# The second block's residual, norms and output projections with tokens on the partitions, its gates as rows read back from a DRAM scratch

## The chip, the cores and the metric

One core of one Trainium2 chip runs the whole model part in one launch. The metric is the device time of one execution in microseconds (us), the median of several executions. Smaller is better.

## The reference

256 tokens of width 1024 pass through two stacked blocks, all in fp32. The first block has two layers of hybrid mixer, memory attention and SwiGLU, each followed by a layer norm. The change leaves its arithmetic alone. The second block runs over a context stream of 256 tokens and over the latents (the first block's output), with adaptive modulation. Cut to what matters here:

```python
def rmsnorm(x, g):
    return x * rsqrt(mean(x * x, axis=-1) + EPS) * g
def modulate(h, shift, scale):
    return h * (1.0 + scale) + shift

for l in range(2):
    sh1, sc1, g1, sh2, sc2, g2 = split(silu(c) @ ada_w[l] + ada_b[l], 6)
    # csh1 ... cg2 in the same way from c_ctx
    h_lat = modulate(rmsnorm(x, norm1_g[l]), sh1, sc1)
    h_ctx = modulate(rmsnorm(ctx, norm1_g[l]), csh1, csc1)
    ...                                   # keys and values of both, attention, branches
    x = x + g1 * (merged @ w_out[l])                             # mixer projection
    h2 = modulate(rmsnorm(x, norm2_g[l]), sh2, sc2)
    x = x + g2 * (hidden(h2) @ ffn_down[l])                      # ffn-down projection
    if l == 0:
        ...                               # the same two updates for ctx, with cg1 and cg2
return x
```

So the second block has six gated residual updates (context layer 0, latent layers 0 and 1; mixer and ffn-down each). Five of them are followed by an rms norm inside the block, and the last one is the output.

## The kernel before

**Products.** The fp32 weights come from DRAM as units of 128x1024 on SyncE's queue into seven `raw` buffers. ScalarE (ACT) copies a unit into `whi`, its high part (L1397, in `hi_part`), GpSimd (POOL) subtracts to get `wlo` (L606), and TensorE (PE) makes each product from three passes: high weight times high input, high weight times low input, low weight times high input. There are four `whi`/`wlo` slots (`SLOTS`). The copy of unit s waits for the raw unit and for unit s-4 to have been used. The order on every engine is written out by hand: PE, ACT and DVE each run through a program of their own, and semaphores join them.

**Two orientations.** With features on the partitions (feature-major) the weights are stationary and 256 tokens are streamed, so a unit is 24 matmuls of 256 columns (`wide_unit`, L640, L641, L644). With tokens on the partitions (token-major) 128 tokens are stationary and 512 weight columns are streamed, so a unit is 12 matmuls of 512 columns (`rows_unit`, L694, L695, L698).

**The first block** has its residual stream token-major already. Its mixer-out and ffn-down projections use `rows_unit`. The last two units go through `last_rows`, which finishes the 256x1024 result piece by piece, (token tile, half) = (0,0), (0,1), (1,0), (1,1). Of these, the first two release `tiles_done` and the last two `units_used`. VectorE (DVE) adds each piece to `x` and takes its statistics (L2026, L2034), ACT takes the root (L1421) and scales 128x256 pieces into `normal` (`normalise`, L1444), PE transposes them (`turn_first`: 8 transposes, `turn_second`: 2 each, L792), ACT writes the high inputs with gain and shift (L1450), and DVE the low ones (L2061, L1964).

**The second block** is feature-major. `mixer_out` and `ffn` use `wide_unit`, the last two units `last_blocks` (four groups of two output tiles, each done before the next begins). `gated_residual` (L2499) is one operation for each of the eight 128x256 tiles: aux times the gate, a per-partition scalar, plus `x`. Then `rms` follows. ACT squares (L1744), PE sums over the partitions (L1200, L1192, L1205), ACT takes the root (L1421), DVE the reciprocal (L2051), PE spreads it (`spread_inverse`, L846), with five `keep_busy` matmuls (L1185) in the waits, and DVE scales each tile (L2480), ACT writes the high input (L1738) and DVE the low one (L2486). The next chunk starts at L657, on `first_hi`, with the first tile.

The latents' first norm of the second block is spread over the context's layer 1: its sums are `latent_sums` (L832). Before it, at the end of the first block, `last_norm` turns the first block's output to feature-major by 16 transposes, and DVE writes `x` (L2069). `DIFF_BEFORE_T` and `DIFF_BEFORE_V` say how many weight units PE works off as cover before each attention step's transposes and values (L1248 among the latter's).

Of the kernel before, what the change touches and what calls it, by code (L numbers as in the profile page):

```python
# [56 lines left out]
PARTS = (0, 1), (2, 3), (4, 5), (6,), (7,)  # L57
# [4 lines left out]
DIFF_BEFORE_T = [1] * STEPS  # L62
DIFF_BEFORE_V = [1, 2, 1, 1] * (STEPS // 4)
# [217 lines left out]
def build(nc, a, split, n_first):  # L281
# [4 lines left out]
    with ExitStack() as ctx:  # L286
# [44 lines left out]
        rows_used = sem("rows_used")  # L331
        ln_var = sem("ln_var")
# [204 lines left out]
        x_first, ln_rows, normal = zt(X_FIRST, 8), zt(LN_ROWS, 8), zt(NORMAL, 8)  # L537
# [17 lines left out]
        def token_moments(tt):  # L555
            return small[:, 88 + 2 * tt:90 + 2 * tt]
# [9 lines left out]

        def scaled_tile(k):
            return aux[:, (2, 3, 1)[k % 3], 0:T]
# [4 lines left out]
        def _(sp):  # L573
# [21 lines left out]
            for q in range(4):  # L595
                sp.wait_ge(out_ready, t.next(out_ready, 2))
                sp.dma_start(a["out"][:, quarter(q)], x[:, quarter(q)]).then_inc(out_sent, 16)
# [11 lines left out]
        def _(pe):  # L609
# [141 lines left out]
            def aux_tile(j):  # L751
                return aux[:, j // 2, (j % 2) * T:(j % 2 + 1) * T]

# [27 lines left out]
            def first_rows(second_half):  # L781
# [8 lines left out]
            def turn(tt, tiles):  # L790
                for k in tiles:
                    mm = pe.transpose(normal_tile(k)[:, tt * P:(tt + 1) * P], normal[:, tt * D + k * P:tt * D + (k + 1) * P], ident)  # L792
                return mm

            def turn_first():
                pe.wait_ge(resid_ready, t.next(resid_ready))
                pe.wait_ge(normal_ready, t.next(normal_ready, 4))
                turn(0, TILES)

            def turn_second(q):  # L800
                pe.wait_ge(normal_ready, t.next(normal_ready))
                turn(1, (2 * q, 2 * q + 1)).then_inc(normal_turned, 1)


            def last_blocks(out, k, h, src):
                xh, xl = src
                wh, wl, low = next_unit()
                low_part(low)
# [2128 lines left out]
```

## Time and profile before

| what | value |
|---|---|
| median of 3 executions | 2621.76 us (2621.74 to 2623.76) |
| profiled execution | 2620.55 us |
| its span (first to last instruction) | 2618.8 us |
| TensorE busy | 2594.7 us, 99% |
| GpSimd busy | 1951.5 us, 75% |
| ScalarE busy | 1431.0 us, 55% |
| VectorE busy | 1213.6 us, 46% |
| granted TensorE clock over the span | 1.000 |

The span is the stretch from the first to the last instruction of the profiled execution. An engine is busy while an instruction of it runs. TensorE's matmuls are pipelined: a matmul's own duration is longer than the distance at which they start, so a run of matmuls is costed by the distance between starts.

### The profile page before, as it was taken

The numbers are of one execution on the slowest core, as the hardware profiler recorded it, in microseconds if no ns is written. First come the engines' busy times: TensorE is split into PE (matmuls) and PEld (weight loads), VectorE is DVE, ScalarE is ACT, GpSimd is POOL, SyncE is SP. The second block draws the span as 40 slices with busy tenths as digits, with TensorE's granted clock in tenths as the row PEclk, the third lists the DMA queues.
The fourth block names the chain that finished last, engine by engine and source line by source line (L and its number), as shares of the span: only waits on it lengthen the run. The fifth ranks groups of instructions, "written<-read, shape, count | busy, mean of one in ns | idle before, by whom it ended". The sixth has DMA issues, their size and how long they took to land.

```text
span 2618.8 us, 42331 instructions
## 1 busy us (share of the span) xinstructions
PE 2594.7 (99%) x16735; PEld 2241.7 (86%) x16735; DVE 1213.6 (46%) x2311; ACT 1431.0 (55%) x2024; POOL 1951.5 (75%) x816
## 2 busy tenths in 40 slices
PE   8999999999999999999999999999999999999999
PEld 8877888889778788888889988887899988878898
DVE  3443462254434553424426552555355554542655
ACT  5756654456565644555654445556554455565443
POOL 6667678876577598786778877865778877568787
PEclk9999999999999999999999999999999999999999
DMA  7556575575566655654455556544445565345453
GB/s 295 211 221 251 165 278 193 188 279 191 212 216 219 257 194 193 236 186 151 163 177 170 189 174 215 191 137 137 164 155 196 185 217 175 133 133 178 165 189 129
DMA packets 139942, 504.60 MB, mean 193 GB/s; under 512 B 15584, under 2 KB 17760, under 8 KB 138080
## 3 DMA queue, kind: packets, MB, share of 16 engines
q1 hardware_dynamic: 132912, 481.57, 53.2%
q10 hardware_dynamic: 6832, 20.32, 2.2%
q8 instruction: 133, 2.18, 0.3%
q14 instruction: 65, 0.53, 0.1%
HBM read 498.68 MB, written 3.15 MB: 192 GB/s over the span
## 4 chain that ended last, share of the span: by engine, by line
PE 94%; DVE 2%; ACT 2%; DVEq 1%; issue 0%; DMA 0%; ACTq 0%; SPq 0%; POOL 0%
PE lin L856 13%; PE lin L644 12%; PE lin L694 12%; PE lin L698 11%; PE lin L695 11%; PE lin L640 5%; PE lin L641 4%; PE aux L644 3%; PE aux L641 3%; PE aux L640 3%; PE aux L695 2%; PE aux L694 2%; PE aux L698 2%; PE aux L1241 1%; PE aux L1259 1%; PE aux L939 1%
## 5 line engine op out<-in xcount | busy, mean ns | idle before, releaser
L606 POOL TENSOR_TENSOR wlo<-raw,whi 128x1024 fp32r<-128x1024 f32 x812 | 1951.3, 2422 | 657.3 <-ACT whi L1397 648.7
L1397 ACT ACTIVATE whi<-raw 128x1024 fp32r<-128x1024 f32 x811 | 845.1, 1057 | 627.6 <-PE lin L698 267.7
L856 PE MATMUL lin<-in_both,whi 128*128 128x512 f32 x1600 | 400.7, 392 | 0.3
L694 PE MATMUL lin<-whi,in_both 128*128 128x512 f32 x942 | 378.1, 401 | 1.5 <-DVE Z L2563 1.2
L695 PE MATMUL lin<-whi,in_both 128*128 128x512 f32 x942 | 367.8, 390 | 0.0
L644 PE MATMUL lin<-in_both,wlo 128*128 128x256 f32 x2560 | 364.4, 283 | 0.3 <-POOL wlo L606 0.3
L644 PEld LDWEIGHTS lin<-in_both,wlo 128*128 128x128 f32 x2560 | 344.8, 191 | 16.4 <-POOL wlo L606 0.7
L856 PEld LDWEIGHTS lin<-in_both,whi 128*128 128x128 f32 x1600 | 289.8, 189 | 55.0 <-DVEq L2441 0.9
L698 PE MATMUL lin<-wlo,in_both 128*128 128x512 f32 x944 | 253.6, 390 | 0.0
L2426 DVE TENSOR_REDUCE Z<-lin 128x512 f32<-128x1024 f32 x100 | 122.4, 1224 | 269.0 <-PE lin L644 267.2
L640 PE MATMUL lin<-in_both,whi 128*128 128x256 f32 x920 | 234.0, 290 | 8.5 <-ACT whi L1902 6.8
L641 PE MATMUL lin<-in_both,whi 128*128 128x256 f32 x920 | 227.9, 284 | 0.0
L694 PEld LDWEIGHTS lin<-whi,in_both 128*128 128x128 f32 x942 | 176.9, 188 | 57.2 <-ACT whi L1397 10.2
L698 PEld LDWEIGHTS lin<-wlo,in_both 128*128 128x128 f32 x944 | 177.1, 188 | 37.8 <-POOL wlo L606 0.3
L695 PEld LDWEIGHTS lin<-whi,in_both 128*128 128x128 f32 x942 | 177.1, 188 | 34.1
L640 PEld LDWEIGHTS lin<-in_both,whi 128*128 128x128 f32 x920 | 176.8, 192 | 21.9 <-issue 10.9
L641 PEld LDWEIGHTS lin<-in_both,whi 128*128 128x128 f32 x920 | 177.0, 192 | 0.3
L694 PE MATMUL lin<-whi,br_hi 128*128 128x512 f32 x360 | 143.7, 399 | 0.0
L695 PE MATMUL lin<-whi,br_lo 128*128 128x512 f32 x360 | 140.5, 390 | 0.0
L640 PE MATMUL aux<-br_hi,whi 128*128 128x256 f32 x528 | 131.4, 283 | 0.0
L641 PE MATMUL aux<-br_lo,whi 128*128 128x256 f32 x528 | 131.4, 283 | 0.0
L1714 ACT ACTIVATE Z<-lin 128x256 f32<-128x256 f32 x60 | 23.1, 384 | 177.4 <-DVEq L2430 177.4
(317 smaller groups left out, 3823.6 us busy)
## 6 DMA issues: line engine op xcount, KB each, us to landing
raw<-in_wstream SPq DMA_DIRECT2D x907, 512.0 KB, 3.3
Z<-in_ln_rows ACTq DMA_DIRECT2D x5, 1024.0 KB, 9.3
gate_row<-in_gate_bias ACTq DMA_DIRECT2D x12, 256.0 KB, 3.2
Z<-in_rel ACTq DMA_DIRECT2D x2, 1536.0 KB, 11.4
Z<-in_mem_t ACTq DMA_DIRECT2D x2, 1024.0 KB, 7.1
kv_store<-Z ACTq DMA_DIRECT2D x2, 1024.0 KB, 8.4
Z<-kv_store ACTq DMA_DIRECT2D x2, 1024.0 KB, 10.7
x<-in_x_tok SPq DMA_DIRECT2D x1, 1024.0 KB, 5.5
```

Of the source, the lines that this page charges most:

```text
L606: pool.tensor_tensor(wlo[s][:, :], raw[i % RAWS][:, :], whi[s][:, :].bitcast(F32), ALU.subtract).then_inc(lo_pool, 1)
L640: pe.matmul(out, wh, xh, start=start, stop=False, skip_group_check=True)
L641: pe.matmul(out, wh, xl, start=False, stop=False, skip_group_check=True)
L644: return pe.matmul(out, wl, xh, start=False, stop=stop, skip_group_check=True)
L694: pe.matmul(out, xh, wh, start=start, stop=False, skip_group_check=True)
L695: pe.matmul(out, xl, wh, start=False, stop=False, skip_group_check=True)
L698: return pe.matmul(out, xh, wl, start=False, stop=stop, skip_group_check=True)
L856: pe.matmul(lin[:, p, up * CH:(up + 1) * CH], wh[:, w], in_both[:, :, k * T:(k + 1) * T], start=(k == 0), stop=(k == KD - 1), skip_group_c ...
L939: mm = pe.matmul(score(g)[tt], q[:, tt * P:(tt + 1) * P], k[:, 0:(tt + 1) * P], start=True, stop=True)
L1241: mm = pe.matmul(aux[:, m, 0:kts * P], q, head_keys(m, h, kts), start=True, stop=True)
L1397: act.activation(whi[s % SLOTS][:, :], raw[i % RAWS][:, :], ACT.Copy).then_inc(hi_ready, 1)
L2426: i = dve.tensor_reduce(three(u, 2), both.rearrange("p a (s t) -> p a t s", s=2), AX.X, ALU.add)
```

## The change

The residual of the second block becomes token-major. Part by part:

- Mixer-out and ffn-down in all three layers of the second block use `rows_unit` and `last_rows`. `wide_unit`, `last_blocks` and `mixer_out` go.
- A gate is now a row along the free axis. For each layer ACT stores both gates to a DRAM scratch (`store_gates`, 2 DMAs, pieces of four values) and loads them back broadcast over the partitions (`load_gates`, 3 DMAs). They lie in the scratch with the feature tile innermost, so DVE reads a gate at a step of four values.
- `gated_residual` is per 128x512 piece a multiplication in place in PSUM and an addition, with a settle behind each. `rms_inverses(0)`, a wait for ACT's root and a reciprocal, stands between the pieces (1,0) and (1,1).
- ACT takes the squares with their sum (`square`), the roots, and scales 128x256 pieces by the inverse (`scale_pieces`). PE turns them (`block_turns`, the last four transposes behind the next chunk's first two units). ACT and DVE modulate the turned tiles.
- PE's sums, `spread_inverse` and three of the five `keep_busy` matmuls go.
- `last_norm` keeps the token-major `x`: its transposes and feature-major tiles go, the row operations of the other norms (`token_rows`) and their 1 MB load take their place. The context is loaded token-major as well (1 MB more).
- `latent_sums` becomes `latent_turns`, 16 transposes.
- One weight unit of the attention's cover moves from before `T(12)` to before `V(11)`.
- The output is token-major and leaves in four quarters, as before, each after one piece.

```diff
-DIFF_BEFORE_T = [1] * STEPS
-DIFF_BEFORE_V = [1, 2, 1, 1] * (STEPS // 4)
+DIFF_BEFORE_T = [1] * 12 + [0] + [1] * 3
+DIFF_BEFORE_V = [1, 2, 1, 1] * 2 + [1, 2, 1, 2] + [1, 2, 1, 1]
...
-            def wide_unit(out, k, kn, src):
-                xh, xl = src
-                wh, wl, low = next_unit()
-                for j in range(KD):
-                    high_product(out(j), wh[:, j * P:(j + 1) * P], tile(xh, k), tile(xl, k), k == 0 and j % 2 == 0)
-                low_part(low)
-                for j in range(KD):
-                    mm = low_product(out(j), wl[:, j * P:(j + 1) * P], tile(xh, k), k == kn - 1)
-                mm.then_inc(units_used, 1)
...
+            def block_turns():
                 pe.wait_ge(lin_free[0], t.ahead(lin_free[0]))
                 keep_busy(2)
-                spread_inverse(0)
-                keep_busy(3)
+                turn_first(block_normal)
+                keep_busy(2)
+                turn_second(0, block_normal)
+                turn_second(1, block_normal)
+            turns_behind = {0: lambda: turn_second(2, block_normal), 1: lambda: turn_second(3, block_normal)}
...
-                mixer_out(lambda: merged_transposes(1))
-                rms()
-                ffn()
+                mixer_rows(lambda: merged_transposes(1))
+                block_turns()
+                ffn(turns_behind)
...
+            def square(src, tt, h, done=None):
+                if done:
+                    act.wait_ge(done, t.next(done))
+                act.activation(token_piece(block_normal, tt, h), token_piece(src, tt, h), ACT.Square, accum_out=piece_squares(tt, h))
+                act.drain()
+                if h:
+                    root(token_std[:, tt:tt + 1], piece_squares(tt, 1), rms_std, 1.0 / D, 0, root_shift(tt))
+                else:
+                    act.activation(root_shift(tt), piece_squares(tt, 0), ACT.Identity, bias=eps[:, 1:2], scale=1.0 / D)
+                    act.drain()
+            def rms(l, x, i, then=None):
+                square(x, 0, 0, resid2)
+                square(x, 0, 1, resid2)
+                square(x, 1, 0, resid2)
+                scale_pieces(x, 0, 0, 2)
+                square(x, 1, 1, resid2)
+                scale_pieces(x, 0, 2, 4)
+                scale_pieces(x, 1, 0, 2)
+                modulated_hi(l, i, 0)
...
+            def store_gates(layer, l, params):
+                act.wait_ge(params_ready, params)
+                stored = a["gate_store"][2 * layer:2 * layer + 2, :].rearrange("g (h p k) -> p g h k", h=2, p=P)
+                for g in range(2):
+                    act.dma_start(stored[:, g], mod[l][:, 24 * g + 16:24 * g + 24].rearrange("p (h k) -> p h k", h=2)).then_inc(gates_stored, 16)
...
-            def gated_residual(l, x, gate, done=resid2):
-                for h in range(2):
-                    for q in quarters_done(2 * h):
-                        for k in (2 * q, 2 * q + 1):
-                            xs = x[:, k * T:(k + 1) * T]
-                            dve.scalar_tensor_tensor(xs, aux[:, k // 2, (k % 2) * T:(k % 2 + 1) * T], mod[l][:, gate + k:gate + k + 1], xs,
-                                                     ALU.mult, ALU.add).then_inc(done, 1)
-                settle()
+            def gated_residual(x, gate, done=resid2):
+                for tt in range(2):
+                    for h in range(2):
+                        if tt:
+                            chunk_done(1)
+                        else:
+                            dve.wait_ge(tiles_done, t.next(tiles_done))
+                        y, xs = rows_bank(tt, h), token_piece(x, tt, h)
+                        tt_(three(y, 4), three(y, 4), gate(h), ALU.mult)
+                        settle()
+                        tt_(xs, y, xs, ALU.add).then_inc(done, 1)
+                        settle()
+                        if tt and h == 0 and done is resid2:
+                            rms_inverses(0)
+                if done is resid2:
+                    settle().then_inc(resid_ready, 1)
+                    rms_inverses(1)
```

How the programs stand against each other at the context's layer 0, between the mixer's projection and the ffn. On PE, before, from the projection's last matmul to the first of the next chunk (`aux` and `lin` are PSUM, `Z` the squares, `c` and `zero_w` constants):

```order
L644 MATMUL aux<-in_both,wlo 128x256
L1200 MATMUL aux<-Z,c 32x256 x6
L1192 MATMUL aux<-c,Z 128x1 x2
L1205 MATMUL aux<-share,probs 128x1 x2
L1192 MATMUL aux<-c,Z 128x1 x2
L1185 MATMUL lin<-zero_w 128x512 x2
L846 MATMUL aux<-c,small 128x128 x2
L1185 MATMUL lin<-zero_w 128x512 x3
L657 MATMUL lin<-in_both,whi 128x256 x4
```

The same place on PE in the changed kernel (`Z` is now the scaled tokens, L794 the transposes, L672 the next chunk's first matmuls):

```order
L713 MATMUL aux<-wlo,in_both 128x512
L1151 MATMUL lin<-zero_w 128x512 x2
L794 MATMUL aux<-c,Z 128x128 x8
L1151 MATMUL lin<-zero_w 128x512 x2
L794 MATMUL aux<-c,Z 128x128 x4
L672 MATMUL lin<-in_both,whi 128x256 x4
L659 MATMUL lin<-in_both,wlo 128x256 x4
```

The sums and the spreading went, and 12 transposes stand ahead of the chunk in their place. Four more follow behind its first two units.

On ACT, before, at the same place (L1397 copies weights, L1744 squares, L1421 is the root, L1738 writes the high inputs):

```order
L1397 ACTIVATE whi<-raw 128x1024 x5
L1744 ACTIVATE Z<-Z 128x512 x3
L1744 ACTIVATE Z<-Z 128x256 x2
L1421 ACTIVATE small<-aux,eps 128x2
L1738 ACTIVATE in_both<-aux,mod 128x256 x4
```

And in the changed kernel (L1353 copies weights, L1398 squares with their sum, L1403 prepares the root and L1377 takes it, L1411 scales, L1712 writes the high inputs):

```order
L1353 ACTIVATE whi<-raw 128x1024 x5
L1398 ACTIVATE Z,small<-Z 128x512
L1403 ACTIVATE small<-small,eps 128x1
L1398 ACTIVATE Z,small<-Z 128x512
L1377 ACTIVATE small<-small 128x1
L1398 ACTIVATE Z,small<-Z 128x512
L1403 ACTIVATE small<-small,eps 128x1
L1411 ACTIVATE Z<-Z,small 128x256 x2
L1398 ACTIVATE Z,small<-Z 128x512
L1377 ACTIVATE small<-small 128x1
L1411 ACTIVATE Z<-Z,small 128x256 x4
L1712 ACTIVATE in_both<-aux,mod,mscale 128x256 x2
```

Between the fifth weight copy and the first high input there were five squares and a root. Now there are four squares, four small operations and six scalings.

## Rows read from the trace of the kernel before

**Rows 1.** The page: busy time of each engine; the chain by engine

```profile
PE 2594.7 (99%) x16735; PEld 2241.7 (86%) x16735; DVE 1213.6 (46%) x2311; ACT 1431.0 (55%) x2024; POOL 1951.5 (75%) x816
PE 94%; DVE 2%; ACT 2%; DVEq 1%; issue 0%; DMA 0%; ACTq 0%; SPq 0%; POOL 0%
```

**Rows 2.** Groups of PE by form: count, then busy us, mean ns

```profile
L640 PE MATMUL aux<-br_hi,whi 128*128 128x256 f32 x528 | 131.4, 283 | 0.0
L640 PE MATMUL aux<-in_both,whi 128*128 128x256 f32 x192 | 49.1, 284 | 0.0
```

**Rows 3.** Timeline of PE: first high matmuls of three units; start us, us

```profile
1342.11 0.39 PE L694 MATMUL lin<-whi,br_hi 128*128 128x512 f32 x1
...
1344.83 0.28 PE L640 MATMUL aux<-in_both,whi 128*128 128x256 f32 x1
...
1347.70 0.28 PE L640 MATMUL aux<-in_both,whi 128*128 128x256 f32 x1
```

**Rows 4.** Timeline of the context's norm between mixer and ffn

```profile
1366.10 1.06 ACT L1397 ACTIVATE whi<-raw 128x1024 fp32r<-128x1024 f32 x1 [1.82 <-PE aux L644]
...
1368.60 0.28 PE L644 MATMUL aux<-in_both,wlo 128*128 128x256 f32 x1
...
1372.99 0.86 ACT L1738 ACTIVATE in_both<-aux,mod 128x256 fp32r<-128x256 f32 x2 [1.24 <-DVE aux L2480]
...
1373.61 0.35 PE L657 MATMUL lin<-in_both,whi 128*128 128x256 f32 x1 [0.53 <-ACT in_both L1738]
```

**Rows 5.** Timeline of two token-major norms of the first block

```profile
885.46 1.63 PE L792 MATMUL aux<-c,Z 128*128 128x128 f32 x10 [1.43 <-ACT Z L1444]
...
1074.70 1.06 ACT L1397 ACTIVATE whi<-raw 128x1024 fp32r<-128x1024 f32 x1 [1.72 <-PE aux L698]
...
1075.57 0.39 PE L698 MATMUL aux<-wlo,br_hi 128*128 128x512 f32 x1
...
1078.30 2.08 ACT L1444 ACTIVATE Z<-x,small 128x256 f32<-128x256 f32 x4 [2.20 <-DVEq L2047]
...
1084.30 1.03 PE L792 MATMUL aux<-c,Z 128*128 128x128 f32 x8
```

**Rows 6.** Prices on ACT and DVE: groups by form; two timeline rows

```profile
L1744 ACT ACTIVATE Z<-Z 128x512 f32<-128x512 f32 x6 | 3.5, 620 | 0.4 <-DVE Z L2499 0.4
L1421 ACT ACTIVATE small<-small,eps 128x1 f32<-128x1 f32 x12 | 3.4, 285 | 1.3 <-DVEq L2039 1.2
...
1706.32 0.64 ACT L1780 ACTIVATE aux<-aux,small 128x512 f32<-128x512 f32 x1
...
1706.98 0.65 ACT L1780 ACTIVATE aux<-aux,small 128x512 f32<-128x512 f32 x1
...
L1964 DVE TENSOR_TENSOR lin<-lin,Z 128x512 f32<-128x512 f32 x16 | 10.4, 694 | 0.6
L2026 DVE SCALAR_TENSOR_TENSOR x<-x,aux 128x512 f32<-128x512 f32 x16 | 10.9, 682 | 21.5 <-PE aux L698 20.6
L1964 DVE TENSOR_TENSOR in_both<-Z,in_both 128x512 fp32r<-128x512 f32 x6 | 9.9, 1675 | 6.2 <-ACT in_both L1418 6.1
```

**Rows 7.** Timeline of PE at the start of the program

```profile
6.76 0.56 PE L640 MATMUL lin<-in_both,whi 128*128 128x256 f32 x1 [6.76 <-ACT whi L1902]
...
9.46 0.41 PE L640 MATMUL lin<-in_both,whi 128*128 128x256 f32 x1
9.67 0.36 PE L641 MATMUL lin<-in_both,whi 128*128 128x256 f32 x1
```

**Rows 8.** Timeline of ACT behind five DMA issues, latent layer 0

```profile
1621.66 2.01 ACT L1397 ACTIVATE whi<-raw 128x1024 fp32r<-128x1024 f32 x2 [5.55 <-issue]
```

**Rows 9.** Timeline of PE: the latents' sums

```profile
1600.35 1.07 PE L832 MATMUL aux<-Z,c 128*32 128x256 f32 x16
```

**Rows 10.** Timeline of DVE: the last residual operations

```profile
2615.33 0.88 DVE L2499 SCALAR_TENSOR_TENSOR x<-aux,mod,x 128x256 f32<-128x256 f32 x2 [0.56 <-PE aux L644]
```

**Rows 11.** Waits of PE: us in total, times, longest

```profile
PE aux L1248 <- DVE probs L2628: 1.5, 2, 0.8
```

More of the change, by code:

```diff
@@ L863, in gate_up, with ffn @@
                         after[k0]()
-            def ffn(after=(), context_norm=False, rows=False):
+            def ffn(after=(), context_norm=False):
                 def down(c):
@@ L868, in down @@
                         pe.wait_ge(hid_lo, t.next(hid_lo))
-                    if rows:
-                        rows_unit(rows_bank, c % 6, c == 0, (br_hi, br_lo))
-                        return
-                    wh, wl, low = next_unit()
-                    high, lower = hidden_tile(br_hi, c), hidden_tile(br_lo, c)
-                    for j in range(KD):
-                        high_product(aux_tile(j), wh[:, j * P:(j + 1) * P], high, lower, c == 0 and j % 2 == 0)
-                    low_part(low)
-                    for j in range(KD):
-                        mm = low_product(aux_tile(j), wl[:, j * P:(j + 1) * P], high, False)
-                    mm.then_inc(units_used, 1)
+                    rows_unit(rows_bank, c % 6, c == 0, (br_hi, br_lo))
                 feature_chunk(0, fresh=TILES, after=after)
@@ L895, in ffn @@
                 pe.wait_ge(hid_lo, t.next(hid_lo, 2))
-                if rows:
-                    last_rows(rows_bank, (HIDDEN - 2) % 6, (br_hi, br_lo))
-                for h in range(0 if rows else 2):
-                    last_blocks(aux_tile, (HIDDEN - 2) % 6, h, (br_hi, br_lo))
+                last_rows(rows_bank, (HIDDEN - 2) % 6, (br_hi, br_lo))
             def modulation_tile(out, u, first, last):
@@ L1145, in first_layer @@
                 last = l == L - 1
-                ffn(columns_behind(fill), last, True)
+                ffn(columns_behind(fill), last)
                 if last:
@@ L1170, in last_norm @@
                 advance(fill, 3)
-                advance(units, 1)
-                turn_first()
-                advance(units, 1)
-                for q in range(4):
-                    turn_second(q)
+                advance(units, 2)
                 advance(fill, 1)
@@ L1437, in token_root, with scale_pieces @@
                 root(token_std[:, tt:tt + 1], token_moments(tt)[:, 1:2], ln_std, 1.0, 0)
+            def square(src, tt, h, done=None):
[8 more added lines that the diff above has]
+                    act.drain()
+            def scale_pieces(src, tt, first, last):
+                if first == 0:
+                    act.wait_ge(rms_inverse, t.next(rms_inverse))
+                for q in range(first, last):
+                    c = slice(tt * D + q * T, tt * D + (q + 1) * T)
+                    act.activation(block_normal[:, c], src[:, c], ACT.Copy, scale=token_scale(tt)).then_inc(normal_ready, 1)
             def normalise(tt, first, last):
@@ L1941, in _ @@
                 modulated_hi(0, 0, k)
+            hi_part()
             evacuate(1, 1, zt(VL + 4, 4))
[L1943 to L1944 removed]
+            for k in range(4, KD):
+                modulated_hi(0, 0, k)
             act.drain().then_inc(kv_copied, 1)
@@ L2325, in first_layer @@
                 residual(rows_bank)
-                rows = norm_with_modulation(l, "ln_ffn", ADA_LN_FFN, not last)
-                if not last:
-                    run(rows)
+                run(norm_with_modulation(l, "ln_ffn", ADA_LN_FFN, not last))
             def context_inverse():
```

240 lines of the change are left out of this document (110 added, 130 removed).

## The prediction

> **What bounds the kernel now.** I read the page first. TensorE is busy 2594.7 of 2618.8 us and makes 94% of the chain that ended last, the other engines have slack [rows 1]. So a change is worth what it takes from TensorE's work, plus what it does to the few stretches where TensorE waits. The table of PE's waits has only short ones past the start (such as [rows 11]), except where the program itself leaves PE with filler. Those places are the norms of the second block. In the timeline of the context's norm the projection's last matmul starts at 1368.60 and its slot of 0.12 ends at 1368.72 (this is T0 below). The next chunk's first matmul starts at 1373.61 [rows 4]. That is 4.9 us in which PE does only sums, spreading and keep-busy matmuls. It is paid five times: context mixer to ffn, start of context layer 1, latent 0 mixer to ffn, start of latent 1, latent 1 mixer to ffn. There the chain is residual, squares, sums, root, spreading, scaling, high input, first matmul. So I cost two things: the projections' matmuls, and the length of that chain.
>
> **Projections.** Before, a 256-column unit takes 1347.70 - 1344.83 = 2.87 us from first matmul to first matmul (24 at 0.12), and a 512-column unit takes 1344.83 - 1342.11 = 2.72 us (12 at 0.227) [rows 3]. There are 528 + 192 = 720 high matmuls at eight to a unit, so 90 units (three layers with 22 + 8) [rows 2]. Each saves 0.15: **-13.6 us**, all on PE's path.
>
> **The norm's new chain, from T0.** Pieces end at -4.1, -2.7, -1.4 and 0 (a quarter of two units, 1.36, apart).
> - DVE takes per piece a multiplication and an addition, 0.69 and 0.68 [rows 6], with settles of about 0.05 each: 1.45. It keeps up. The last piece, behind the wait for the first tile's root (2.2, below) and its reciprocal, is added by about 3.9.
> - ACT is the question. Its fifth weight copy waits for a slot. Before, half of the last two units was freed 2.6 us ahead of T0 (1366.10 against 1368.72). In `last_rows` both are held until the third piece is done. The first block shows that: 1074.70 against a last matmul that starts at 1075.57 [rows 5]. So the copy runs from -1.1 to about 0, and every square stands behind it, though the first two pieces were ready long before.
> - A square with its sum is 0.66 (starts 1706.32 and 1706.98, an exponential of the same size with its sum; the plain square has 0.62), a 128x1 operation 0.285 [rows 6], and I take 0.1 for a drain. Two pieces of one token tile are then 1.10 + 1.05. A scaling of 256 columns has a cadence of 0.50 (four in 2.08, the last 0.59) [rows 5].
> - In program order: squares of tile 0 until 2.2, square (1,0) 3.3, two scalings 4.3, square (1,1) with root 5.4, two scalings 6.45, two more 7.4. PE's eight transposes start at 6.5 and take 0.9 (8 in 1.03, the last one's latency off [rows 5]), two keep-busy matmuls bring it to 7.9, two transposes 8.1, ACT's first high input (0.59 by the 256-column scaling) 8.8, the first fresh matmul about 8.9.
>
> Against 4.9 that is +4.0, five times: **+20 us**. No PE work lies beside it: unlike the first block's norms, `block_turns` has only 4 keep-busy matmuls.
>
> **Behind it in the chunk.** Four transposes, about 0.45. DVE's path to the low input is a pass longer (`tensor_scalar` and subtraction, where one operation stood). A 256-column pass takes 0.44 (two in 0.88 [rows 10]), so the low inputs come about 0.5 later, and DVE then needs about 0.95 for a tile where PE needs 1.44: a wait at the first tile or two, 0.7 in all. Five times 1.15: **+5.8 us**.
>
> **The latents' first norm.** 16 transposes, about 1.9 us, and perhaps 1 us of wait, against sums of about 1.5 (the largest of them 1.07 [rows 9]): **+1.4**. **`last_norm`** loses 16 transposes, two runs of eight at 1.03 with latency [rows 5]: **-1.9**. Its DVE work (token rows, more than the tiles it replaces) and its 1 MB load lie beside the second block's first chunks, and I put them at 0. What they need late is the context's residual only, hundreds of us on.
>
> **The end.** The last two tiles take 0.88 on DVE behind the last matmul [rows 10]. The new piece takes 1.45: **+0.5**. The output's transfers stay.
>
> **The clock.** At the program's start PE idles for 6.76 us and then starts 256-column matmuls 0.21 us apart until 9.67 (9.46 and 9.67 [rows 7]), where 0.12 is the full rate [rows 3]: the 1.2 GHz level for 14 matmuls, 1.3 us lost. Nowhere else is PE idle over 1.5 us (1.43 at 885.46 [rows 5], without a slow stretch behind it). The new norm leaves PE idle from about 0.5 to 6.5, nearly as long as at the start, with ten small matmuls to follow. I take the same 1.3 us for each, on transposes, keep-busy matmuls and first tiles: **+6.5**. The bounds are 0 and 1.9 (transposes slowed inside the chain as well) each, 0 to 9.5.
>
> The Trainium skill states the same rule ("TensorE: Matmul & The Clock Gate", section "Why this matters for your kernels"): gaps between bursts of matmuls put the engine back to the lower clock. By it all five norms lose clock. The start's rows agree, though they show a cold start and not a gap in a run, which is why the term has a chance and isn't taken as sure.
>
> **Gates.** DVE reads the gate at a step of four values. The trace has no such read. Below: it costs as the contiguous one, 0.69. Above: as a 512-element pass with two SBUF operands and POOL beside it, 1.68 [rows 6], so +1 per piece. As ACT binds until the squares of tile 1, the first three pieces have cover; only the last piece (needed at 4.3) and the end of the kernel would feel it: up to +0.7 five times and +1 three times, +6. I take 0.
>
> The Trainium skill ("SBUF — State Buffer", section "Specifications (TRN2)") says that each access which crosses to a new 16-byte line pays a penalty. A step of four fp32 values does that each time, so by it the multiplication is slower than the contiguous one.
>
> The DMAs for the gates are five more issues on ACT per layer. At the start of latent layer 0 five issues in a row kept ACT from everything else for 5.55 us, and no wait of PE followed, since four slots of weights stand between [rows 8]. The two stores join exactly that crowd, 2.2 us at 1.1 each: 0 to 2.2 more for PE. I take 0, as now. The moved unit of cover stands at a place where PE waits up to 0.8 now [rows 11]: -0.8 to +1.5, taken as 0.
>
> **Sum.** -13.6 + 20 + 5.8 + 1.4 - 1.9 + 0.5 = +12.2, with the clock +18.7. On the profiled execution's 2620.55 that is 2632.8 and 2639.3. The median of the runs is 1.2 above it: 2634.0 and **2640.5 us**.
>
> **Rivals.**
> - *Chain as forecast, no clock drop*: 2634. For it: the granted clock reads 1.000 over the whole span although the start is slow, so the rows tell little of the gate, and the keep-busy matmuls stand on both sides. Chance 0.22.
> - *The other side, the chain stays short*: if the weight copy were not late, ACT had the first three squares behind it before T0, and the last piece bound: 1.45 for DVE, square and root 1.05, reciprocal with its settle 0.2, one scaling 0.5, transposes 0.3, high input 0.6, first matmul 0.1, so 4.2 to 4.6, as short as today's 4.9. At 4.6 the sum is -13.6 - 1.9 + 1.4 + 0.5 + 5 x (1.15 - 0.3) = -9.3, **2612**. The sign turns where a norm is 1.6 us longer than today, since 5 x (1.6 + 1.15) makes up the 13.6 that is left without the norms. Against it: from the end of the copy ACT's own work alone is 7.4, whatever DVE does. Chance 0.15, and 0.08 more for a case between, within 0.2%.
> - *A slower multiplication, gate DMAs or attention cover on top*: 2640 + 6 to 10, **2648**. Chance 0.15.
> - The change does what it says as far as the order shows, so a case of "nothing happens" isn't among them.
>
> My forecast (chain and clock) has 0.40. From the cases: faster by over 0.2% (5 us, about what a measurement of this kernel can tell) 0.15, within it 0.08, slower 0.77. For 8 in 10 the range drops the fast rival and the far end: **2621 to 2651**. The likeliest case alone would have 2635 to 2646.
>
> **What the profile after would show.** Units of the projections 2.72 apart. The fifth weight copy ending at about T0, the last scaling ahead of the first high input ending near +7.4, PE idle of about 6 us before the eight transposes, released by ACT's scaling. First fresh matmul at +8.9. Behind it matmuls of 256 columns 0.21 apart for some 3 us if the clock fell, 0.12 if not. Multiplication by the gate near 0.69. I am wrong if the gap is under 7 us (squares ahead of the copy, or drains and sums cheaper), if PE has waits elsewhere that I put at 0, or if the gate's read is far above 0.69.

## The result and the profile after

The changed kernel takes **2651.43 us** (median of 4, 2650.92 to 2651.85), the kernel before 2621.99 us beside it. The ratio is 1.0113, with a 95% interval of [1.0101, 1.0125]: slower by 29.4 us. The sign was forecast. The time lies 0.4 us above the stated range, and the loss is 1.6 times the 18.7 that were forecast. The profiled span is 2648.9 us against 2618.8, so 30.1 us are to be found.

The page after, its busy line and its chain, beside [rows 1]:

```profile
PE 2585.9 (98%) x15578; PEld 2190.2 (83%) x15578; DVE 1243.1 (47%) x2307; ACT 1459.5 (55%) x2109; POOL 1954.1 (74%) x816
PE 92%; DVE 2%; ACT 2%; DMA 1%; POOL 1%; DVEq 1%; ACTq 1%; issue 0%; SPq 0%
```

TensorE is busy 9 us less, and the kernel is 30 us longer: the loss is idle time. The changed kernel's waits of PE (us in total, times, longest) say where:

```profile
PE aux L794 <- ACT Z L1411: 29.5, 6, 5.7
...
PE lin L709 <- ACT whi L1353: 4.5, 2, 3.4
PE lin L837 <- DVEq L2431: 3.4, 3, 1.1
...
PE lin L713 <- POOL wlo L621: 1.8, 5, 0.5
```

Five waits of 5.7 us stand ahead of the eight transposes of the five norms. This is the timeline of the context's norm after, at the place of [rows 4]:

```profile
1368.40 1.06 ACT L1353 ACTIVATE whi<-raw 128x1024 fp32r<-128x1024 f32 x1 [3.02 <-PE aux L713]
...
1369.28 0.39 PE L713 MATMUL aux<-wlo,in_both 128*128 128x512 f32 x1
1369.37 0.61 ACT L1398 ACTIVATE Z<-Z 128x512 f32<-128x512 f32 x1
...
1373.04 0.69 DVE L1966 TENSOR_TENSOR Z<-aux,Z 128x512 f32<-128x512 f32 x1
1373.77 0.63 ACT L1398 ACTIVATE Z<-Z 128x512 f32<-128x512 f32 x1
...
1374.76 1.69 ACT L1411 ACTIVATE Z<-Z,small 128x256 f32<-128x256 f32 x4
...
1375.80 1.94 PE L794 MATMUL aux<-c,Z 128*128 128x128 f32 x8 [5.68 <-ACT Z L1411]
1377.53 1.06 PE L1151 MATMUL lin<-zero_w 128*128 128x512 bf16 x2
1378.38 1.06 PE L794 MATMUL aux<-c,Z 128*128 128x128 f32 x4
...
1379.76 0.71 PE L672 MATMUL lin<-in_both,whi 128*128 128x256 f32 x4 [0.32 <-ACT in_both L1712]
```

The last slot ends at T0 = 1369.51. The fifth weight copy ends at T0, the squares follow in a row, and the transposes start at +6.3, as forecast. But the eight then take 1.94 us where the first block's take 1.03 [rows 5], the filler 1.06, and the first fresh matmul comes at **+10.25** (forecast 8.9, before 4.9). The reason shows in the windows of that norm (the busy times, then the granted clock, DMA share and GB/s at the end):

```profile
1369.50:1372.60 3.10, 0.61 (x3) 0.12 (x2) 2.63 (x4) 2.54 (x9) 2.37 (x1) 1.00 0.33 128
1372.70:1379.40 6.70, 3.60 (x14) 2.74 (x14) 1.12 (x3) 3.96 (x11) 0.00 (x0) 0.50 0.24 79
1379.50:1384.00 4.50, 4.01 (x31) 3.82 (x32) 3.63 (x8) 3.54 (x8) 1.20 (x1) 0.99 0.02 4
```

The granted clock fell to 0.50 (1.2 GHz) 2.6 us into the idle stretch, and it was back at 2.4 GHz 0.2 us before the first fresh matmul. All five norms have such a slow stretch of 6.8 us, beginning 2.6 to 4.7 us into the idle time. In the other four it ends behind the first fresh matmul: 0.1 us behind it at the start of latent layer 1, and 1.7 to 1.9 us in three norms. Two windows around its end in the second norm, where the first fresh matmul starts at 1575.76:

```profile
1577.25:1577.50 0.25, 0.25 (x2) 0.25 (x1) 0.25 (x1) 0.25 (x2) 0.00 (x0) 0.50 0.00 0
1577.50:1577.75 0.25, 0.25 (x2) 0.17 (x2) 0.25 (x2) 0.25 (x2) 0.00 (x0) 0.92 0.00 0
```

The first fresh matmul comes at +10.25 in all five, so most of the loss lies on the norm's own chain. What the slow clock costs in the chunk behind is priced with e1_busy below.

**Where the 30.1 us are.** The start of the same PE work in both traces, subtracted, gives a shift; its growth between two places is what that stretch costs.

| stretch | forecast | measured |
|---|---|---|
| `last_norm` and the context's first chunks (shift +2.0 at 1220) | -1.9 | +2.0 |
| projections, 90 units at 0.15 | -13.6 | -13.6 |
| the five norms, T0 to first fresh matmul (10.25 - 4.89 each) | +20 and clock 6.5 | +26.8 |
| chunks behind four of the norms (three ffns 1.9, 2.0, 2.1; latent 1 1.1) | +4.6 | +7.1 |
| chunk behind the context's second norm, latents' norm | +1.2 and +1.4 | +2.0 |
| start of latent layer 0 | 0 | +4.7 |
| moved cover (the two waits of 0.8 at L1248 [rows 11] are gone) | 0 | -1.8 |
| behind the last matmul | +0.5 | +2.9 |

They sum to 18.7 and 30.1.

### The profile page after: what moved, and what is told of

Its sections match the earlier page's. It is cut to its first block, busy times and chain, and to the rows that moved or that the text cites. A ratio compares the mean times of both kernels' runs of the same rounds, so it can differ in the third digit from the quotient of the medians.

```text
span 2648.9 us, 40235 instructions
## 1 busy us (share of the span) xinstructions
PE 2585.9 (98%) x15578; PEld 2190.2 (83%) x15578; DVE 1243.1 (47%) x2307; ACT 1459.5 (55%) x2109; POOL 1954.1 (74%) x816
## 4 chain that ended last, share of the span: by engine, by line
PE 92%; DVE 2%; ACT 2%; DMA 1%; POOL 1%; DVEq 1%; ACTq 1%; issue 0%; SPq 0%
PE lin L837 13%; PE lin L709 11%; PE lin L659 11%; PE lin L713 11%; PE lin L710 11%; PE aux L710 5%; PE aux L709 5%; PE aux L713 5%; PE lin L655 4%; PE lin L656 4%; DMA raw<-in_wstream 1%; PE aux L1190 1%; PE aux L1208 1%; PE aux L907 1%; PE aux L875 1%; PE aux L794 1%
## 5 line engine op out<-in xcount | busy, mean ns | idle before, releaser
L1353 ACT ACTIVATE whi<-raw 128x1024 fp32r<-128x1024 f32 x811 | 845.2, 1057 | 621.3 <-PE lin L713 266.1
L710 PE MATMUL aux<-whi,br_lo 128*128 128x512 f32 x440 | 172.5, 392 | 0.0
L709 PE MATMUL aux<-whi,br_hi 128*128 128x512 f32 x440 | 172.2, 391 | 0.0
L713 PE MATMUL aux<-wlo,br_hi 128*128 128x512 f32 x440 | 122.5, 389 | 0.0
```

The source lines that it names most:

```text
L709: pe.matmul(out, xh, wh, start=start, stop=False, skip_group_check=True)
L710: pe.matmul(out, xl, wh, start=False, stop=False, skip_group_check=True)
L713: return pe.matmul(out, xh, wl, start=False, stop=stop, skip_group_check=True)
L1353: act.activation(whi[s % SLOTS][:, :], raw[i % RAWS][:, :], ACT.Copy).then_inc(hi_ready, 1)
```

## The experiments

All medians are of 4 to 11 executions, beside the kernel before on the same chip (2621.2 to 2622.0).

### e1_busy: no idle stretch ahead of the transposes

```diff
                 pe.wait_ge(lin_free[0], t.ahead(lin_free[0]))
-                keep_busy(2)
+                keep_busy(26)
                 turn_first(block_normal)
```

> Edit: 26 instead of 2 filler matmuls ahead of the eight transposes, in each of the five norms, so that PE has no idle stretch there. Clock theory: the eight transposes take about 1.06 instead of 1.94 and the filler behind them 0.6 instead of 1.06, the first fresh matmul comes 8.9 instead of 10.25 behind the projection's end, the granted clock is 1.000, and the time falls by about 5 x 1.35 = 6.8, to 2644.7. Rival (the slow stretch is harmless since most of it lies in idle time, the chain on ACT sets the gap): no change, 2651. Rival (the filler's 5.7 us reach past the ready transposes): slower by up to 0.3 a norm.

Measured: 2643.38 us, 8.1 less than the changed kernel. The timeline of PE at the same norm:

```profile
1368.45 0.39 PE L713 MATMUL aux<-wlo,in_both 128*128 128x512 f32 x1
1368.68 5.79 PE L1151 MATMUL lin<-zero_w 128*128 128x512 bf16 x26
1374.99 1.06 PE L794 MATMUL aux<-c,Z 128*128 128x128 f32 x8 [0.52 <-ACT Z L1411]
1375.89 0.59 PE L1151 MATMUL lin<-zero_w 128*128 128x512 bf16 x2
1376.32 0.60 PE L794 MATMUL aux<-c,Z 128*128 128x128 f32 x4
1377.45 0.71 PE L672 MATMUL lin<-in_both,whi 128*128 128x256 f32 x4 [0.53 <-ACT in_both L1712]
```

The transposes take 1.06 and the gap is 8.77, the forecast's 8.9. The clock theory holds: with PE busy the norms have no slow stretch, and 1.48 us come back in each. The other 3.9 per norm are the chain itself, as forecast. Behind the third and the fifth norm, where the changed kernel's slow stretch reached 1.7 and 1.9 us into the chunk, the work up to the next norm or the end is only 0.20 and 0.25 us shorter here. (The profile has one slow stretch elsewhere, at 1636, behind the wait of 3.5 us at the start of latent layer 0. The changed kernel's profile has none there, and the work around it is 2.2 us longer here.)

### e2_order: ACT's work in another order

The fifth weight copy moves from ahead of the squares to behind the scalings, and the first tile's scalings to ahead of the last square:

```diff
-                hi_parts(5)
+                hi_parts(4)
                 rms(l, x, 1, ACT.Silu)
...
                 square(x, 0, 1, resid2)
-                square(x, 1, 0, resid2)
                 scale_pieces(x, 0, 0, 2)
-                square(x, 1, 1, resid2)
+                square(x, 1, 0, resid2)
                 scale_pieces(x, 0, 2, 4)
+                square(x, 1, 1, resid2)
                 scale_pieces(x, 1, 0, 2)
+                hi_part()
```

> Edit on ACT alone: the fifth weight copy is issued behind the scalings instead of ahead of the squares, and all four scalings of the first token tile stand ahead of the last square. Theory (ACT's order of work sets the gap): the eight transposes start about 4.5 us behind the projection's end instead of 6.3, the first fresh matmul 1.3 to 1.8 us earlier in each norm, together 2651.4 - 5 x 1.35 = 2644.7. Rival (DVE, at 1.9 us for each piece, has become the bound): the last piece is added 4.2 behind the end whatever ACT does, and the gap shrinks by under 0.5 each, 2649 or more. Rival (the next chunk then waits for the weight that is copied late): no gain.

Measured: 2645.99 us, 5.4 less, between the theory (2644.7) and its rival (2649). The gap shrank to 9.1 to 9.5, by 0.8 to 1.1 each. The order matters, but the first square of the second half isn't free: the second piece is added on DVE only at T0, and DVE's reciprocal stands behind the third piece's addition (1.9 us a piece).

### e3_issues: DMA issues behind the weight copies

The two gate stores and the load of the context rows are issued behind the layer's gelu instead of at its start.

```diff
-                store_gates(layer, l, (1, 3, 4)[layer])
                 act.dma_start(zt(S2, 2), a["sgu_w"][l * P:(l + 1) * P, :]).then_inc(sgu_landed, 16)
...
                 act.drain().then_inc(gelu_ready, 1)
+                store_gates(layer, l, (1, 3, 4)[layer])
+                if not layer:
+                    act.dma_start(context, a["ctx_tok"]).then_inc(ctx_tok_landed, 16)
```

> Edit: the stores of the gates and the load of the context rows are issued later in a layer, behind the copies of the first weights and the gelu. Theory (DMA issues in front of weight copies on ACT): the waits of 3.4 us at 1640 and of 1.0 us at 1094 go, 2651.4 - 4.4 = 2647.0, perhaps with 0.3 given back where the issues now stand. Rival (the transfers themselves are late or crowd the weights' queue): the waits stay or show as waits for raw, 2650 to 2651.

Measured: 2647.76 us, 3.7 less. This is what had happened in the changed kernel at the start of latent layer 0, where [rows 8] were free of a wait:

```profile
1633.77 2.55 ACTq L1739 DMA_DIRECT2D gate_store<-mod  x2
1636.34 1.35 ACTq L1820 DMA_DIRECT2D Z<-in_sgu_w  x1
1637.72 1.22 ACTq L1821 DMA_DIRECT2D Z<-in_sgu_b  x1
1638.97 0.46 ACTq L1822 DMA_DIRECT2D Z<-in_lam  x1
1639.54 3.90 ACT L1353 ACTIVATE whi<-raw 128x1024 fp32r<-128x1024 f32 x4 [6.93 <-issue]
...
1640.74 0.47 PE L709 MATMUL lin<-whi,in_both 128*128 128x512 f32 x1 [3.44 <-ACT whi L1353]
```

With the edit the wait is 1.59 and the one near 1094 (1.03) is 0.27. The rest of 1.59 is no matter of the gates: ACT reaches the remaining issues later against PE than in the kernel before (first store issued 7.5 us behind the chunk's first fresh matmul, where it was 3.1), since the last high inputs wait for transposes that stand behind PE's units. So the 3.44 are 1.85 for the two stores and 1.59 for the later place.

### e4_rows: the last norm's row operations later

```diff
-                run(norm_with_modulation(l, "ln_ffn", ADA_LN_FFN, not last))
+                rows = norm_with_modulation(l, "ln_ffn", ADA_LN_FFN, not last)
+                if last:
+                    return rows
+                run(rows)
...
                     qk_chunk(c, rotate, gating_lo if c == 0 else None)
+                    if not rotate and c < 3:
+                        advance(last_token_rows, (2, 1, 1)[c])
```

In this kernel the row operations read a normalised tile that the query chunks have written over by then, so the latents' values differ. The instructions and their sizes are the same.

> Edit on DVE alone: the four row operations of the first block's last norm run between the context's query and key chunks instead of beside its first chunk. Theory (they slow POOL's subtractions beside them from 2.4 to 2.9 to 3.3 us, with no spare slots at that place): the four waits of PE for wlo behind 1094 (0.55, 0.31, 0.33, 0.32) go, 2651.4 - 1.5 = 2649.9. Rival (the slots are short because ACT's copies start 1 us late there, whatever DVE does): the waits stay, 2651.4.

Measured: 2650.34 us, 1.1 less; the span is 1.5 less, and four waits for wlo behind 1094 are gone. In the changed kernel POOL's subtractions beside the row operations stand so:

```profile
1093.81 17.38 POOL L621 TENSOR_TENSOR wlo<-raw,whi 128x1024 fp32r<-128x1024 f32 x6 [8.31 <-ACT whi L1353]
...
1094.27 3.27 DVE L1966 TENSOR_TENSOR x<-x,Z 128x1024 f32<-128x1024 f32 x1
...
1096.51 1.20 PE L713 MATMUL lin<-wlo,in_both 128*128 128x512 f32 x4 [0.55 <-POOL wlo L621]
```

Six in 17.38 is 2.9 each, over the 2.72 in which PE uses a unit.

### e5_gate: the gates contiguous

```diff
-            return row.rearrange("p (f k) -> p k f", k=4)
+            return row.rearrange("p (k f) -> p k f", k=4)
...
-                stored = a["gate_store"][2 * layer:2 * layer + 2, :].rearrange("g (h p k) -> p g h k", h=2, p=P)
+                stored = a["gate_store"][2 * layer:2 * layer + 2, :].rearrange("g (h k p) -> p g h k", h=2, p=P)
```

> Edit: the gates lie in the scratch in plain feature order (the stores have pieces of one value), so DVE reads them contiguously. Theory (the step of four values costs 1.07 instead of 0.69 for each piece, and it counts only where DVE is last): the multiplication takes 0.69, the tail behind the last matmul shortens by about 1.5, the norms' gap stays at 10.25 since ACT is last there, 2651.4 - 1.6 = 2649.8. Rival (the slow gate read is what made the norms long): the gap shrinks by 0.4 to 1.5 in each, 2643 to 2648. Rival (1024 pieces of 4 bytes for each gate come late or hold ACT's queue): a new wait, 2651 or more.

Measured: 2663.86 us, 12.4 more. In the changed kernel the gate's read shows as

```profile
L1966 DVE TENSOR_TENSOR aux<-aux,ytok 128x512 f32<-128x512 f32 x12 | 12.8, 1068 | 30.7 <-PE aux L713 29.8
```

and here as 699 ns. The norms' gap went from 10.25 to about 9.9. But the stores of single values held ACT's queue in the context's layer 0. The two stores there in the changed kernel, then the same place here:

```profile
1090.14 0.94 ACTq L1739 DMA_DIRECT2D gate_store<-mod  x2
```

```profile
1089.11 5.33 ACTq L1739 DMA_DIRECT2D gate_store<-mod  x2
1094.47 4.30 ACTq L1820 DMA_DIRECT2D Z<-in_sgu_w  x1
1098.80 2.40 ACTq L1821 DMA_DIRECT2D Z<-in_sgu_b  x1
1101.23 0.46 ACTq L1822 DMA_DIRECT2D Z<-in_lam  x1
1101.78 3.90 ACT L1353 ACTIVATE whi<-raw 128x1024 fp32r<-128x1024 f32 x4 [11.43 <-issue]
...
1102.98 0.77 PE L709 MATMUL lin<-whi,in_both 128*128 128x512 f32 x1 [11.17 <-ACT whi L1353]
```

So the second rival was right: the stores in pieces of one value took 5.33 for two, against 0.94 with pieces of four, and the next issues were longer too. In the profile the first norm comes 8.8 later, and the stretches with the starts of the latents' two layers are 3.4 and 4.3 longer. The tail is 1.5 shorter, as the theory had it.

### e6_short: only what the first tiles need

```diff
+                pe.wait_ge(normal_ready, t.next(normal_ready, 2))
+                turn(0, (0, 1), block_normal)
                 keep_busy(2)
-                turn_second(0, block_normal)
-                turn_second(1, block_normal)
+                pe.wait_ge(resid_ready, t.next(resid_ready))
+                turn(0, (2, 3), block_normal)
+                pe.wait_ge(normal_ready, t.next(normal_ready, 2))
+                turn(1, (0, 1), block_normal).then_inc(normal_turned, 1)
+                pe.wait_ge(normal_ready, t.next(normal_ready))
+                turn(1, (2, 3), block_normal).then_inc(normal_turned, 1)
```

> Edit on ACT and PE: the fifth weight copy behind the first two high inputs, only the scalings that the first two feature tiles need ahead of them, PE turns those tiles as they come (2 + 2 + 2 + 2 transposes ahead of the chunk, the others in pairs behind its first two units). The gate's read stays at a step of four. Theory (the gap is the ordering of ACT's work plus the clock): the last piece is added 4.2 behind the end, its square, root and one scaling end at about 6.0, first fresh matmul near 7.0 instead of 10.25, 2651.4 - 5 x 3.2 = 2635. If PE's idle stretches of 2 to 3 us still bring the clock down, 0.5 to 1 more for each norm, 2638 to 2640. Rival (the chain has a floor of its own, drains and semaphores): gap above 8.5, 2643 or more.

Measured: 2642.79 us, 8.6 less where 11 to 16 were expected, though the gap did shrink to 7.5 (by 2.75 each). The stretches between the norms gave about 7 us back. The windows of its second norm show it (first fresh matmul at 1569.78):

```profile
1563.00:1566.00 3.00, 0.00 (x0) 0.00 (x0) 2.64 (x5) 1.95 (x6) 0.00 (x0) 1.00 0.38 150
1566.00:1569.70 3.70, 2.22 (x10) 1.25 (x10) 0.57 (x3) 3.11 (x9) 0.00 (x0) 0.67 0.00 0
1569.80:1572.80 3.00, 3.00 (x7) 2.42 (x8) 2.76 (x7) 3.00 (x7) 1.69 (x1) 0.50 0.00 0
1573.00:1576.00 3.00, 3.00 (x15) 2.44 (x14) 0.68 (x3) 1.83 (x4) 2.34 (x2) 0.82 0.50 157
```

The slow stretch began behind a shorter idle time, and then lasted into busy PE time (until 1574.09). So a shorter gap with the same slow stretch behind it can move the loss from idle time to work. Not all of the 7 us is shown to be that: 3.9 of them lie between the second and the third norm, where this profile also has the slow stretch at 1636 that e1_busy has and the changed kernel hasn't. How much is the clock's, e9_short_busy shows.

### e7_best: the edits together

The reordered norms, contiguous gates, later issues, and the row operations spread where their inputs still stand (two ahead of the context's gating, two behind its first query chunk).

> Edit: the reordered norms of the run before this one, the contiguous gates, the later DMA issues, and the last norm's row operations spread over the context's first chunks. Theory (all measured terms add up): the gap of a norm 5.5 to 6.0 (DVE's last piece at 1.6 to 2.2 behind the end), 2651.4 - 5 x 4.4 - 1.6 - 3.6 - 1.1 = 2623, the same as before the change within 0.2%; if the chunk's follow-up waits (1.1 three times) go too, 2620. Rival (another engine binds once these are gone): gap of 7 or more, 2630.

Measured: 2631.66 us (2628.77 to 2635.37), 19.8 less, ratio to before 1.0039 [1.0026, 1.0052]. That is 8.7 over the expected 2623. The gap is 5.9 to 6.4, above the 5.5 to 6.0 expected, and each norm still has a slow stretch.

### e8_proj: the kernel before with the new projections alone

```diff
-                    wide_unit(aux_tile, k, KD, (in_hi, in_lo))
+                    rows_unit(rows_bank, k, k == 0, (in_hi, in_lo))
...
-                for h in range(2):
-                    last_blocks(aux_tile, KD - 2, h, (in_hi, in_lo))
+                last_rows(rows_bank, KD - 2, (in_hi, in_lo))
```

> The kernel before, with one edit: the second block's projections run as 12 matmuls of 512 columns with tokens stationary, everything behind them unchanged (the residual then reads a transposed result, so the output isn't the reference's, the instructions and waits are those of before). It prices the first term alone. Theory (0.15 for each of 90 units, the norms about 0.5 longer as the last two slots come free later): 2622.0 - 13.6 + 0 to 2.5, 2608.4 to 2611. Rival (units come no faster since another engine paces them): over 2615.

Measured: 2613.45 us, ratio 0.9970 [0.9958, 0.9981], 8.2 less than before, over the expected 2611. Its profile says why: between two norms the 22 units of the context's ffn take 3.32 us less (0.15 each, the term is right), and the norms are 1.05 longer (gap 5.94; one of the five 6.22), twice what I had allowed for the later last slots.

### e9_short_busy, e10_best_busy: the same two with PE kept busy

The counts are 18 and 7 in e9_short_busy, 13 and 7 in e10_best_busy.

```diff
-                keep_busy(2)
+                keep_busy(18)
                 pe.wait_ge(normal_ready, t.next(normal_ready, 2))
                 turn(0, (0, 1), block_normal)
-                keep_busy(2)
+                keep_busy(7)
```

> Edit: the reordered norms of the run e6_short with 18 and 7 filler matmuls where they have 2 and 2. Theory (in e6_short the half-rate stretch of 3.4 or 6.8 us began later against the norm and so fell on the next chunk's matmuls, which gave back about 7 us of what the order had gained): with PE kept busy there is no slow stretch, the gap is 6.6 to 6.9 instead of 7.5, the chunks behind lose nothing, 2642.8 - 9 to 11 = 2632 to 2634. Rival (the loss behind the norms is ACT's and DVE's, not the clock's): only the gap shrinks, 2639 or more.

Measured: 2638.16 us, 4.6 less than e6_short, short of the expected 9 to 11. No norm has a slow stretch, but the gap stayed at 7.2 to 7.5, so PE's rate doesn't set it there. DVE's pieces do, as the next runs show. Of the 7 us that e6_short had lost between the norms, 4.0 came back. The other 3.4 stayed. Behind the first norm that is 0.4, the same in both runs, with no slow stretch behind it in either, so the rival was right for a part: some of the loss belongs to the new order of work on ACT and DVE. (One slow stretch of 3.4 us is left between the norms, at the start of latent layer 0.)

> Edit: e7_best with 13 and 7 filler matmuls where it has 2 and 2. Theory: gap 5.5 to 5.8 instead of 5.9 to 6.4, no slow stretch in or behind the norms, 2631.7 - 5 to 8 = 2624 to 2627, still slower than before the change by 0.1 to 0.2%, since the gap stays over the 4.9 of before and the transposes and waits of the chunks are extra. Rival (the spread of e7_best, 2628.8 to 2635.4, has another cause): no change, 2630.

Measured: 2626.81 us, 4.9 less than e7_best, ratio to before 1.0020 [1.0010, 1.0029]. No norm has a slow stretch, but the gap is 6.0 to 6.4 as in e7_best, and not the 5.5 to 5.8 of the theory. The two profiled executions differ by only 1.7, since e7_best's was its shortest (2628.77), so where the rest of the 4.9 lies isn't shown.

### e11_strided: the slow gate read in the short norm

> Edit: e10_best_busy with the gates back at a step of four values (stores with pieces of four values, 18 filler matmuls for 13). It prices the gate's read where DVE is last. Theory (0.38 for each piece, three to four pieces on the path of each norm and of the end): gap 1.0 to 1.3 longer five times, the tail 1.5, the small waits from the 4-byte stores about 1 less: 6 to 7 us over e10_best_busy. Rival (ACT is last even in the short norm): gap as in e10_best_busy, at most 2 us over it.

The kernel is e10_best_busy with the gates at a step of four again, and 18 filler matmuls for 13. Measured: 2631.95 us, 5.1 more than e10_best_busy, a little under the expected 6 to 7. The gaps are 7.2 to 7.5 against 6.0 to 6.4. Once ACT's order is short, DVE is last, and then the step of four counts in every norm. (The profiled execution was a long one, with a span of 2637.4 and a wait of 4.4 at 1129 behind a DVE operation that took 6.79 where e10_best_busy has 1.42. Only its gaps are used.)

### e12_copy_ahead: POOL's run out of DVE's way

```diff
                 for k in range(4, KD):
+                    if k == 6 and ahead:
+                        hi_part()
                     modulated_hi(l, i, k)
```

with one copy less in the run that follows.

> Edit on e10_best_busy, ACT's order alone: one weight copy of the next four is moved ahead of the last two high inputs of each norm (ACT sits idle there for 2.1 us, waiting for the last transposes). Theory (the later copies shift POOL's run of subtractions onto DVE's product of two SBUF operands, which takes 1.67 instead of 0.75 and makes PE wait 1.1 in each of the three ffns; and the first weight behind the latents' norm comes 1.6 late): POOL's run of four ends 2.4 us earlier, the product takes about 0.75, the three waits of 1.1 go to 0.3, the wait of 1.56 goes, 2626.8 - 2.4 - 1.6 = 2622.8, not told from the 2621.7 before the change. Rival (DVE's product is slow for another reason, such as its place in the buffer): the product stays at 1.67 and only the latents' wait goes, 2625.2. Rival (the copy waits for a slot that isn't free, and holds the high inputs): slower, 2628 or more.

Measured: **2620.29 us** (11 executions), ratio to before 0.9998 [0.9989, 1.0007], 6.5 less than e10_best_busy. DVE's product in the ffn, before, in the changed kernel and here:

```profile
L1964 DVE TENSOR_TENSOR Z<-Z 128x512 f32<-128x512 f32 x3 | 2.2, 743 | 2.2 <-ACT Z L1702 2.2
```

```profile
L1966 DVE TENSOR_TENSOR Z<-Z 128x512 f32<-128x512 f32 x3 | 5.0, 1658 | 2.2 <-ACT Z L1674 2.2
```

```profile
L1985 DVE TENSOR_TENSOR Z<-Z 128x512 f32<-128x512 f32 x3 | 2.1, 693 | 2.2 <-ACT Z L1685 2.2
```

In the changed kernel it stands at 1398.64 inside POOL's run from 1390.24 to 1399.76. Here POOL's run ends at 1390.4 and the product starts at 1391.66. The three waits of 1.1 are down to 0.2, and each ffn is 1.0 shorter. The wait of 1.56 is gone. The 6.5 are more than the 4.0 expected: a wait of 1.4 at 1674 that e10_best_busy's profile has in latent layer 0 isn't here, and nothing shows that the edit removed it.

## Why the prediction was right and wrong

**Right: what bounds, the sign, the projections, the chain.** 0.15 a unit held to the hundredth (e8_proj). The steps of the norm came within 0.2 us as long as the clock was full: copy until T0, transposes at 6.3 (6.5 forecast), gap 8.77 in e1_busy (8.9). One premise was wrong without harm to the sum: "the first two pieces were ready long before". DVE had added the second only at T0 (1368.79 and 0.69), which fits what moving the copy gave in e2_order: 0.8 to 1.1 a norm, where 1.3 to 1.8 were expected. The Trainium skill's "TensorE: Matmul & The Clock Gate", section "Why this matters for your kernels", says that gaps between bursts of matmuls bring the lower clock; all five norms show it, and it was the case that I had put first.

**The clock, right in kind, a little small.** I took 1.3 from the program's start and its bound of 1.9; 1.48 was measured. Its place was wrong in part: I put it on the first tiles too. The half rate did reach them in four of the five norms, by 0.1 to 1.9 us, but it cost little there (0.2 behind two of them, by e1_busy). The loss lay on transposes and filler inside the chain.

**Wrong: the terms that I put at 0.** The text said of the gate DMAs: "The two stores join exactly that crowd, 2.2 us at 1.1 each: 0 to 2.2 more for PE. I take 0, as now." They took 2.55, and PE waited 3.44: the slots that had been spare in [rows 8] were not, since ACT comes to this place 4 us later against PE than before. It was a term with known crowding taken at its lower bound, and the cover was read from the old order. The stretch cost +4.7 where I had 0. Of the wait of 3.44, e3_issues took back 1.85, within the range of 0 to 2.2, and 1.59 is ACT's lateness, for which the forecast had no term. The remaining 1.3 wasn't taken apart by a run.

**Wrong: `last_norm`.** "Its DVE work (token rows, more than the tiles it replaces) and its 1 MB load lie beside the second block's first chunks, and I put them at 0." DVE had room, but POOL did not: beside the row operations its subtractions take 2.9, over PE's 2.72 for a unit, at a place where ACT had started late. Together with the issues ahead of the first copy, the step of -1.9 became +2.0. e3_issues and e4_rows took back 0.8 and 1.5 of it. The rest, a wait for raw weights of 1.0 and some tenths, wasn't tried.

**Wrong: the end.** I costed one piece behind the last matmul. At 1.9 us a piece DVE falls behind PE's 1.36 from the first piece on, so the whole lag of four counts: it had added the last piece 3.7 behind the last matmul, and +0.5 became +2.9. With contiguous gates (e5_gate) 1.5 of that was gone. The same sentence, "it keeps up", failed in the norms, where ACT hid it. The gate's read was put at 0.69 and took 1.07, between the two bounds. The Trainium skill's "SBUF — State Buffer", section "Specifications (TRN2)", has the penalty for each new 16-byte line; the trace agrees, 1068 against 699 ns.

**Mis-sized: the chunks.** The forecast had transposes and late low inputs, +1.15. In the three ffns 2.0 were measured, 1.1 of it a wait that I hadn't named: the product above, doubled by POOL's later run. e12_copy_ahead shows it.

**Unforeseen gain.** The moved cover took both waits at L1248, -1.8. I had said -0.8 to +1.5.

So the mechanism that decides was forecast, and the miss of 11 us is a sum of side terms: 4.7 + 3.9 + 2.4 + 2.5 + 0.3 - 0.6 - 1.8.

**What the change is worth.** Its gain, 13.6, is real, and the chain on ACT eats it. With ACT's order, the clock, the issues, the gates' order and POOL's place mended, the token-major version stands level with the kernel before (0.9998), not ahead: its gap is still 6.0 to 6.4 against 4.9, which takes 6.0 of the gain in the five norms. By the two profiles about 8 more go in the work behind them, 1.4 in each of the first two ffns and 2.9 in the last with the tail.

## What to carry to other kernels

When the one busy engine must wait for a chain on others, cost that chain in the program order of its slowest engine, and look at what that engine does just before it: here a weight copy, released late, put every square behind the end. A stretch that makes the main engine idle can cost twice, once as time and once at half rate, and shortening it without filling it can move the slow stretch onto real work. Don't price an added DMA issue, or work on an engine with slack, at nothing because today's trace shows cover: cover is the spare slots at that place in the new order, and two engines can slow each other, as DVE's product of two SBUF operands did with 1658 ns beside POOL's run and 693 ns without it.

## What the hardware showed that I hadn't expected

- The slow stretches that begin in the norms took 6.8 us in all five norms of the changed kernel, and 3.4 us in two and 6.8 us in three norms of e6_short. In the changed kernel the clock was up again between 0.2 us before and 1.9 us behind the first fresh matmul; in three norms of e6_short it was down through the chunk's first 3.5 to 4.3 us.
- The same wait can come with and without a slow stretch: the one of 3.4 us at 1640 has none in the changed kernel, and in e2_order a wait of 3.4 us at the same place has one of 3.4 us.
- A DMA issue's time on ACT depends on the pieces of the one before it. Behind the stores of single values the plain load of `in_sgu_w` took 4.30 us, otherwise 0.49 at that place.
